# Moving the gate's reciprocal root on GpSimd, and shifting three steps of a Mamba-2 group by one to three weight pieces

## The reference, cut to what matters

```python
def mamba2_mixer(h, ...):
    zxbcdt = h @ w_in                       # z 4096 | x 4096, B 1024, C 1024 | dt 64
    xbc = silu(causal_depthwise_conv(xbc))  # 4 taps over tokens
    dt = softplus(dt + dt_bias);  a = -exp(a_log)
    y = ssd_scan(xs * dt, dt * a, bm, cm)   # chunks of 64: (C B^T * decay) @ x, and a carried state
    y = y + xs * d_skip
    g = y * silu(z)
    g = g * rsqrt(mean(g * g over the group's 512 channels) + EPS) * out_norm_w   # the gate's norm
    return g @ w_out
```

## Time and profile before

| | us |
|---|---|
| median of 3 runs | 2434.57 (2433.26 to 2435.48) |
| the profiled execution: its time | 2434.61 |
| the profiled execution: its span | 2432.5 |
| PE busy in the span | 2403.2 (99%) |
| DVE busy | 1957.5 (80%) |
| ACT busy | 1283.8 (53%) |
| POOL busy | 269.4 (11%) |

### The profile page before, as it was taken

How to read it: one execution, slowest core, us unless ns; L and a number is a source line. 1 busy time by engine, 2 the same in 40 slices (tenths; PEclk the granted TensorE clock), 3 DMA queues, 4 the chain that set the end, 5 groups by cost and what they waited for, 6 DMA issues and landing times.

```text
span 2432.5 us, 31340 instructions
## 1 busy us (share of the span) xinstructions
PE 2403.2 (99%) x11459; PEld 1998.8 (82%) x11459; DVE 1957.5 (80%) x2211; ACT 1283.8 (53%) x1544; POOL 269.4 (11%) x434
## 2 busy tenths in 40 slices
PE   8999999999999999999999999999999999999999
PEld 8888788878888888888888888888888888888887
DVE  6888888876569889889889866666689899898897
ACT  5555555554445545455455655555555555455453
POOL 1111111110101001011011111101110010010010
PEclk9999999999999999999999999999999999999999
DMA  7787778776887667668577765555887677677684
GB/s 226 212 238 234 233 234 241 241 244 214 238 248 234 221 216 244 211 212 268 178 240 232 243 208 188 179 183 174 257 260 232 196 247 218 224 233 225 199 254 161
DMA packets 290801, 543.79 MB, mean 224 GB/s; under 512 B 22958, under 2 KB 56080, under 8 KB 289664
## 3 DMA queue, kind: packets, MB, share of 16 engines
q1 hardware_dynamic: 264736, 457.87, 59.4%
q0 software_dynamic: 25664, 84.31, 12.1%
q10 hardware_dynamic: 288, 0.11, 0.0%
HBM read 502.29 MB, written 39.91 MB: 223 GB/s over the span
## 4 chain that ended last, share of the span: by engine, by line
PE 82%; DVE 7%; issue 4%; DMA 4%; ACT 2%; POOL 1%; DVEq 0%; ACTq 0%; SPq 0%; POOLq 0%
PE acc L692 14%; PE acc L693 14%; PE acc L694 14%; PE acc L517 6%; PE acc L519 6%; PE acc L518 6%; PE aux L518 3%; PE aux L517 3%; PE aux L519 3%; PE aux L718 2%; PE aux L720 2%; PE aux L719 2%; DVE w_lo L1303 2%; PE acc L718 2%; PE acc L719 2%
## 5 line engine op out<-in xcount | busy, mean ns | idle before, releaser
L1085 ACT ACTIVATE w_hi<-w_raw 128x1024 fp32r<-128x1024 f32 x392 | 415.0, 1060 | 496.4 <-PE acc L694 384.1
L1303 DVE TENSOR_TENSOR w_lo<-w_raw,w_hi 128x1024 fp32r<-128x1024 f32 x353 | 426.9, 1220 | 230.7 <-ACT w_hi L893 230.1
L692 PE MATMUL acc<-w_hi,stationary 128*128 128x512 f32 x1564 | 609.2, 390 | 0.0
L693 PE MATMUL acc<-w_lo,stationary 128*128 128x512 f32 x1564 | 608.5, 389 | 0.0
L694 PE MATMUL acc<-w_hi,stationary 128*128 128x512 f32 x1564 | 608.5, 389 | 0.0
L1624 DVE TENSOR_TENSOR w_lo<-w_raw,w_hi 128x1024 fp32r<-128x1024 f32 x392 | 476.2, 1220 | 123.7 <-ACT w_hi L1085 118.3
L893 ACT ACTIVATE w_hi<-w_raw 128x1024 fp32r<-128x1024 f32 x353 | 368.2, 1056 | 263.5 <-PE acc L519 126.4
L517 PE MATMUL acc<-w_hi,stationary 128*128 128x512 f32 x960 | 378.1, 394 | 2.6 <-DVE w_lo L1303 2.6
L518 PE MATMUL acc<-w_lo,stationary 128*128 128x512 f32 x960 | 373.8, 389 | 0.0
L519 PE MATMUL acc<-w_hi,stationary 128*128 128x512 f32 x960 | 373.8, 389 | 0.0
L692 PEld LDWEIGHTS acc<-w_hi,stationary 128*128 128x128 f32 x1564 | 293.6, 188 | 63.5 <-DVE w_lo L1624 2.9
(11 more groups left out here) (249 smaller groups left out, 2893.8 us busy)
## 6 DMA issues: line engine op xcount, KB each, us to landing
w_raw<-in_w_up SPq DMA_DIRECT2D x200, 512.0 KB
w_raw<-in_w_down SPq DMA_DIRECT2D x192, 512.0 KB
w_raw<-in_ssm_w_in SPq DMA_DIRECT2D x129, 512.0 KB
w_raw<-in_ssm_w_out SPq DMA_DIRECT2D x64, 512.0 KB
work<-in_w_down SPq DMA_DIRECT2D x64, 512.0 KB
w_raw<-in_w_kv SPq DMA_DIRECT2D x64, 512.0 KB
work<-in_w_up SPq DMA_DIRECT2D x56, 512.0 KB
spread<-work POOLq DMA_DIRECT2D x44, 512.0 KB, 4.6
```

The costliest lines, as they stand in the source:

```text
L692: pe.matmul(o, xh, hi[:, k], start=starts[t] and k == 0, stop=False)
L693: pe.matmul(o, xh, lo[:, k], start=False, stop=False)
L1085: a.activation(whi[:, unit % RING, :], raw[:, slot, :], ACT.Copy).then_inc(sem("hi_made"), 1)
L1303: v.tensor_tensor(wlo[:, s, :], raw[:, pos.raw_slot(off), :], whi[:, s, :].bitcast(F32), ALU.subtract).then_inc(sem("lo_made"), 1)
```

## The change

It moves work; the computation stays the same.

- GpSimd: `x_raw_spread` is split into `x_raw_away` (out to HBM) and `x_raw_back` (back), and `gate_rstd(g-1)` stands between them.
- ScalarE and VectorE, `tail`: the last tap and `conv_x` go from j = 0 (and 1) to 1 (and 2); the first tanh and its product from 2 to 3; the mask product from 3 to 6; the second tanh from 3 to 4, its product and turn from 4 to 5; the gate's normalising and turn from 18 to 19.
- The exponents (L1530) go from j = 17 to 16; `gate_hi` and `gate_lo` of group g-2 from j = 5 to 4.
- Output product: the tail's steps no longer skip i = 8, so its steps from 8 on come one piece sooner, with `scan` after i = 10 and not 11; the last `gate_hi`/`gate_lo` go from i = 24 to 25.

```diff
 # TensorE, output product
-                if i == 11:
+                if i == 10:
                     scan(GROUPS - 1, GROUPS)
 # ScalarE, tail
-                if j == 0:
+                if j == 1:
                     a.wait_ge(sem("x_raw_turned"), r * 64 + 64)
                     ...
-                if j == 2:
+                if j == 3:
                     a.wait_ge(sem("x_conv_lin"), r * 4 + 2)
                     ...
-                if j == 3:
+                if j == 4:
                     a.wait_ge(sem("x_conv_lin"), r * 4 + 4)
                     ...
-                if j == 18:
+                if j == 19:
                     a.wait_ge(sem("g_rstd"), r + 1)
 # ScalarE, group (gate_hi) and VectorE, group (gate_lo)
-                    if j == 5 and not first and not second:
+                    if j == 4 and not first and not second:
 # ScalarE and VectorE, output product
-                if i == 5:
+                if i == 4:
                     gate_hi(GROUPS - 2)
-                if i != 8:
-                    tail(i if i < 8 else i - 1, GROUPS - 1)
-                if i == 24:
+                tail(i, GROUPS - 1)
+                if i == 25:
                     gate_hi(GROUPS - 1)
 # VectorE, tail
-                if j in (0, 1):
-                    conv_x(r, 2 * j)
-                if j == 2:
+                if j in (1, 2):
+                    conv_x(r, 2 * (j - 1))
+                if j == 3:
                     v.wait_ge(sem("x_tanh"), r * 2 + 1)
                     ...
-                if j == 3:
+                if j == 6:
                     v.wait_ge(sem("decay_made"), r + 1)
                     v.wait_ge(sem("cb_masked"), r + 1)
                     ...
-                if j == 4:
+                if j == 5:
                     v.wait_ge(sem("x_tanh"), r * 2 + 2)
                     ...
-                if j == 18:
+                if j == 19:
                     v.wait_ge(sem("g_normed"), r + 1)
 # VectorE, group
-                    if j == 17:
+                    if j == 16:
                         v.wait_ge(sem("row_in"), g * 16 + 16)
 # GpSimd
-            def x_raw_spread(g):
+            def x_raw_away(g):
                 gp.wait_ge(sem("raw_squares"), g + 1)
                 gp.dma_start(x_raw_dram..., cvx...).then_inc(sem("x_raw_out"), 16)
+            def x_raw_back(g):
                 gp.wait_ge(sem("x_raw_out"), g * 16 + 16)
                 ...
-                x_raw_spread(g)
+                x_raw_away(g)
                 gate_rstd(g - 1)
+                x_raw_back(g)
                 g_out(g - 1)
                 g_back(g - 1)
```

More of the change, by code:

```diff
@@ L2038, in _ @@
             mask_cb(0)
-            x_raw_spread(0)
+            x_raw_away(0)
+            x_raw_back(0)
             for g in range(1, GROUPS):
```

## The result

Thirteen runs of each kernel gave a median of 2442.17 us for the changed kernel (2432.34 to 2447.7) and 2434.57 us for the one before (2432.42 to 2436.39). The ratio is 1.0027, with a 95% interval of 1.0015 to 1.0039: slower by 0.27%, where 2412.9 us, 0.9% faster, had been forecast, and 2421 had been the upper end of the range. The profiled execution took 2442.98 us, span 2440.9, 8.4 us longer than the span of before.

The account below looks back on a forecast made before the run. PE was taken to bound the kernel (busy 2403.2 of 2432.5 us). Removing waits for w_lo gives 15.2 + 3.4 = 18.6 us, less waiting of scan 3.1: 2434.6 - 21.7 = 2412.9 us, range 2409 to 2421.

Parts of the forecast that it names:

- What bounds the kernel, and what the waits cost: PE bounds; its waits at L532 (15.2 us), L517 (3.4) and before scan (5.9), restarts included, are all that can be won: 24.5.
- The root takes 0.72 us: On GpSimd, the gate's reciprocal root ahead of the raw x fetches runs 316.4 to 317.1, so fetches begin 1.2 us later.
- The last fetch lands 4.5 us after its issue: Raw x's last fetch, issued at 318.9, lands at 323.4, or 7.0 us after issue at most, at 325.9.
- fourth rival: GpSimd waits for g_ms, raw x misses the tap; each us beyond 9.7 costs 7; 2439 us at 13.7; chance 0.04.
- Gate: back 3.5 to 5.2 us after out: On GpSimd, the gate's way back begins 3.5 to 5.2 us after g_out; the last part lands at 330.8 to 334.2.
- The turn ends 0.5 to 1.2 us behind piece 4: VectorE's turn, which starts the trip to HBM and back, ends 0.5 to 1.2 us after PE begins piece 4.
- VectorE's queue from turn to j = 10 is 13 us: VectorE's queued work from the turn to the step at j = 10 takes 13 us, for 14.9 in group 2 before.
- `scan` keeps 2.8 us of waits: PE's wait at L607: 0.7 us in three groups, 0.1 in a fourth, 0.16 each added; 2.8 stay, 3.1 go.
- second rival: Gate's data come late, the turn ends 1.2 us behind piece 4, scan waits 1.3 us per group: 2418.9 us; chance 0.17.
- The granted clock: TensorE's clock had no term in the sum; a wait before scan was priced at its bracket plus 0.16 us.

Follow-up runs that it names:

- Experiment 9: Changed kernel with weight loads of pieces 1 to 4 in every group but the first cut to a part: 2417.47 us, 0.9928.
- experiment 15: Changed kernel with fetches ahead of the root, gate_hi at piece 5, gate_lo at 5 behind turn and product, mask product at 8: 2416.45 us, 0.9924.
- experiment 2: Kernel before with only the root moved between raw x's way out and way back: 2431.55 us, 0.998.
- experiment 12: Changed kernel with the exponents back at piece 17, behind g_ms: 2430.18 us, 0.9975.
- experiment 13: Kernel before with the root between raw x's way out and back and the mask product at piece 6: 2423.43 us, 0.9953.
- experiment 6: Changed kernel with fetches of raw x ahead of the root, and gate_hi and gate_lo at piece 6 instead of 4: 2421.1 us, 0.9949.
- experiment 1: Changed kernel with the root put back behind the four fetches of raw x on GpSimd: 2431.81 us, 0.9969.
- experiment 8: Kernel before with VectorE doing the skip product twice instead of once: 2452.25 us, 1.0074.
- experiment 10: Kernel before with only the steps of tap, convolution, tanh and products moved one piece on: 2440.56 us, 1.0026.
- experiment 3: Changed kernel with scan one piece later, in the groups and in the output product: 2465.88 us, 1.013.

## Why the prediction was wrong

Its steps in their order:

- *What bounds the kernel, and what the waits cost:* held. The waits of L532 and L517 went, as said, except 1.8 us in 2; the longer, 1.16 us, is in group 2, whose tap came 0.24 us after piece 0. Normalising no longer waits for the root.
- *The root takes 0.72 us:* it took 1.61 to 1.63 us, all seven times that it stood before fetches. The earlier trace rows showed it with VectorE idle beside it; the change put it beside a `lo`. 0.9 us too little, but g_ms came 0.8 us sooner than taken (the root starts 12.1 us before piece 0, for 11.4), so the fetches were off by 0.2 us only.
- *The last fetch lands 4.5 us after its issue:* this is the step that failed. Taken was the median of the earlier trace rows, and 7.0 as the worst, from the first fetch 6.3 and 8.8 us. The tap started 8.7 to 9.9 us after the first fetch in all seven groups (8.1 in the output product), at most 0.2 us after the last landing, having waited 2.4 to 4.4 us. Two things went wrong. That median is over all four fetches of a batch, and the tap needs the slowest: asked for one batch at a time, the tile's view shows that the slowest took 5.0 to 7.0 us in the kernel before, 6.7 to 8.8 from the first fetch, though only the tap of group 1 waited for it. Group 5, before and after:

```profile
DMA to landing us min/median/max: 4.0/4.2/5.8
```

```profile
DMA to landing us min/median/max: 5.0/5.7/6.8
```

  In this group 7.6 us were on record for 6.3 taken, and the change added another 1.0. Experiment 9 gives the forecast's own numbers for tap and turn once the loads are thin, and takes the time to 2417.47. The fourth rival named this place with its price (from 9.7 us after the first fetch each us costs 7 us) but looked for the cost in w_lo, which still came in time, and not in the turn. It had 0.04.
- *Gate: back 3.5 to 5.2 us after out:* in after it is 7.1 to 8.8 us, so `gate_hi` waited 1.0 to 1.7 us. That cost the turn nothing, as forecast: `gate_hi` was over 1.0 to 1.7 us before the second tanh could start, since that had to wait for VectorE.
- *The turn ends 0.5 to 1.2 us behind piece 4:* 2.9 to 3.3. The stretch from the tap to the turn was right (16.25 us, for 16.2 to 16.9), so all of the difference is the tap's lateness.
- *VectorE's queue from turn to j = 10 is 13 us:* 13.1 where the trip let it. Held. From turn to L1474 it took 13.1 to 17.4 us, for 15.35 taken, and PE waited long where the trip was long; its longer values do not go away with the loads of pieces 1 to 4 thinned (18.6 in group 5 of experiment 9), and why this group has them stays open.
- *`scan` keeps 2.8 us of waits:* 19.2. The second rival (1.3 us in each group, at 0.17) was right in kind and place, at under half the size, and had the turn late for the gate and not for raw x.
- *The granted clock:* not in the sum at all. In the earlier trace rows `scan` never waits long enough to lose it, so the forecast priced a wait at its length plus 0.16 us. It cost 10 to 12 us here.

Forecast against measured in the profiled execution: 2443.0 - 2412.9 = 30.1 us. The wait of `scan` gives 19.2 - 2.8 = 16.4, the clock 10.3 to 12.0, what is left of L532 2.3 (1.8 and two restarts): 29.0 to 30.7.

A gain nearly as large as forecast was there, in another order: 0.76% in experiment 15 (2416.45 us), for 0.9%.

## What to carry to other kernels

A landing that nobody waits for has been given slack, not a duration: take the slowest part of each batch and not the median of all parts, bound it by the longest that somebody did wait for, add the spread of its issues, and ask which loads the same change lets start sooner. When work is moved closer to its consumer, go down the queue behind every wait that it gains (here VectorE's row, 16.25 us from the tap to the turn) until the next round trip, and price what the trip's consumer then does at its own longest value. A wait on the way, as that of `gate_hi`, costs only what its own followers wait for it. And price a wait of the matmul engine of more than some 2 us above its length, since the clock may fall behind it; moving one step at a time showed which of the three parts lost what the other two had won.

## What the runs showed of the hardware

- *An operation of two columns on GpSimd* (the root) took 0.71 to 0.72 us with VectorE idle, 1.61 to 1.63 us beside a `lo` of 1.23 us in after, and 2.67 to 2.68 us beside the exponents of 2.29 us (experiments 2, 12 and 13). In every run, a root that starts while such an operation of VectorE has more than 0.2 us to go ends 0.56 to 0.58 us behind that operation: in group 5 of after this `lo` is over at 317.69 and the root at 318.26. A root that had started first took its 0.72 us, beside a `lo` that began 0.03 us later and took 1.26 (experiment 6). The Trainium skill, page SBUF — State Buffer, section "SBUF: two separate sides", says that a VectorE operation with two SBUF inputs may hold the port pair shared with GpSimd; this trace agrees for an operation that reads and writes SBUF.

```profile
316.46 1.23 DVE L1302 TENSOR_TENSOR w_lo<-w_raw,w_hi 128x1024 fp32r<-128x1024 f32 x1
```

- *The issue of a DMA on GpSimd* did not stretch: 582 to 643 ns in 32 issues of after, some beside such operations of VectorE. The same section's statement that descriptors may wait for the port, which it makes of VectorE's two-port mode, did not show in any run here.

```profile
L2022 POOL DMA_DIRECT2D work<-x_raw x32: 582/586/643, 68.6 to 512.5; - x32
```

- *TensorE's granted clock* fell from 1.00 to 0.50 (2.4 to 1.2 GHz) in or after waits of 1.9 to 5.1 us ahead of the small products of `scan`, and stayed there 3.4 or 6.8 us. It never fell at a wait of `scan` of 1.8 us or less, nor at six of 1.9 to 2.9 us in experiments 1, 6, 8 and 10; it fell at every one of 3.1 us or more. Ahead of another product (L660, experiment 3) it fell at one of 1.80 us.
- *The landings of the fetches of raw x* went with what else was under way: 3.3 us in the median with thin loads, 4.5 in the kernel before, 5.5 in the changed one. The slowest of each batch of four took 5.0 to 7.0 us before and 6.3 to 7.9 after.
